# Three stages between the products: the step sizes and two head norms each move beside a product

## The chip, the cores and the metric

The kernel is one program on one core of a Trainium2 chip. The time is device microseconds of that core, for one call. The engines named below are PE (TensorE, matrix products; PEld is its weight load), ACT (ScalarE), DVE (VectorE), POOL (GpSimd) and SP (SyncE, which here issues the loads of weights).

## The reference, cut to what matters

The program computes three transformer layers in float32. The change touches the mixer of the third, which has two branches over the same normed tokens (H): an attention branch with output O and a state-space branch (a scan) with output Y. This is what the touched stages compute, written from the kernel:

```
O   = differential_attention(H)                 # 8 heads of 128 features, 512 tokens
O   = O / rms_over_each_head(O) * subln * 0.8   # the attention's head norm: 8 groups of 1 tile
dt  = softplus(H @ w_dt + dt_bias)              # 32 step sizes for each of 768 tokens
a   = -exp(a_log) * dt; its sums up to, after and over each chunk; exp of the sums
for g in 4 groups:
    B, C, x = silu(conv3(H @ xbc[g]))           # 4 tiles of 128 features
    Y[g] = scan(B, C, x, dt, the sums)          # uses dt and the sums from its first step on
Y   = Y * silu(H @ z)
Y   = Y / rms_over_groups_of_256(Y) * ssd_norm  # the scan's norm: 4 groups of 2 tiles
YA  = (O @ w_ba) * sigmoid(H @ gates[0:8])
YS  = (Y @ w_bs) * sigmoid(H @ gates[8:16]) + YA
```

Behind it come the output product, a router, experts and their combination.

## The kernel before, in words

All activations lie feature by feature: a tile is 128 features (partitions) by up to 512 latent and 256 context tokens. The program is a list of stages, built by `plan` (L2930). Each stage has one method for each engine. Behind each stage every engine signals that it is done and waits until all four are (`run` in `build`, L3020 to L3037; L3035 is the wait, and the profile writes DVEq L3035 or ACTq L3035 for whoever came last). So nothing of one stage overlaps the next, but for one thing: SP isn't held by this meeting. It runs ahead and loads weights into a ring of 8 slots of 512 KB as soon as PE has used what lay there (`ring_loads`, L202, whose issue is L211; it waits on `unit_used`).

The stages around the change, in order, with their lines:

- `DiffAttention` (L1762), which ends at ACT L1921.
- `GroupNorm` on O (L1620): for each of 8 groups ACT squares (L1673), PE multiplies by a matrix of ones to sum over the partitions (L1654), ACT takes the root (L1679), and DVE inverts it (L1695), multiplies by 0.8 (L1698) and scales the tile (L1702). Buffers are doubled.
- `StepSizes` (L1941): PE forms 48 small products (L1969, 128x32 out); DVE computes the softplus as a chain of short instructions (L2011 to L2042), with one exponential by ACT (L2001, L2002); PE forms 11 products for the sums (L1981); DVE copies them (L2044) and spreads them (L2047), ACT takes the exponentials (L2004), DVE weighs (L2050), PE turns four tiles (L1995) and DVE copies them out (L2052). Its 8 ring slots all hold `w_dt`.
- Four times `ConvLinear` (L991) and `Scan` (L2060). `ConvLinear` has 4 units here; a unit is one ring slot and one output tile: 8 products of 512 columns and 8 of 256 (L1021). ACT copies the tile (L1049), DVE convolves it (L1062, L1065, L1070), ACT takes silu (L1042). PE's unit j needs what ACT took of unit j-2.
- `GatedLinear` with z (L1707): 8 units of 8 products (L1729), ACT's silu (L1742), DVE's product (L1751).
- `GroupNorm` on Y: 4 groups of two tiles.
- `Linear` with `w_ba` (L459): 8 units (L500), ACT's copy (L516). Then `GatedLinear`, `Linear`, `GatedLinear` again.

A product of float32 stands as two records in the trace, so 8 products of a unit are 16 records. The order of the work on each engine is the order in which the methods issue it; there is no scheduler. ACT holds one table of functions at a time, and `ACT_TABLE_LOAD` is put straight ahead of the instruction that needs another one.

Of the kernel before, what the change touches and what calls it, by code (L numbers as in the profile page):

```python
# [27 lines left out]
P = 128  # L28
# [158 lines left out]
class Stage:  # L187
    def sync(self, sp): pass
# [270 lines left out]
class Linear(Stage):  # L459
# [3 lines left out]
    def __init__(self, k, w, n_tiles, rhs, dst, kt=KD, spans=(LAT, CTX), func=ACT.Copy, t0=0, d0=0, scale=1.0):  # L463
# [22 lines left out]
    def tensor(self, pe):  # L486
        k, upt = self.k, self.upt

        def unit(i, j):
# [13 lines left out]
            mm.then_inc(k.sig("unit_used").sem, 1)  # L503

        run_body(pe, self.n_units, self.body, unit)

    def scalar(self, act):
        k, upt = self.k, self.upt

        def unit(i, j):  # L510
            if j % upt != upt - 1:
                return
            t = j // upt
            act.wait_ge(k.sig("unit_used").sem, self.u0 + j + 1 + i * self.body)
# [3 lines left out]
            a.then_inc(k.sig("out_taken").sem, 1)  # L518

        run_body(act, self.n_units, self.body, unit)  # L520

# [469 lines left out]
class ConvLinear(Stage):  # L991
# [3 lines left out]
    def __init__(self, k, w, n_tiles, dst, cw, cb, off, spans=(LAT, CTX), pair=True, t0=0, head=()):  # L995
# [13 lines left out]
    def sync(self, sp):  # L1009
        ring_loads(self.k, sp, lambda i, j, c: self.w[i + j + self.t0, :, 0:c], self.u0, self.n)  # L1010

    def tensor(self, pe):
        k = self.k

        def unit(i, j):
# [7 lines left out]
            mm.then_inc(k.sig("unit_used").sem, 1)  # L1023

        run_body(pe, self.n, 8, unit)

    def scalar(self, act):
# [16 lines left out]
        def unit(i, j):  # L1044
# [6 lines left out]
            silu(i, j)  # L1051

        run_body(act, self.n, 8, unit)

    def vector(self, dve):
# [17 lines left out]

        for j, raw in enumerate(self.head):
# [7 lines left out]
        def unit(i, j):  # L1082
# [6 lines left out]
            if self.pair and j % 2 == 1:  # L1089
# [3 lines left out]
                                  self.cv[:, (j - 1) % 4, 0:self.end], self.cv[:, j % 4, 0:self.end], ALU.mult)  # L1093

        run_body(dve, self.n, 8, unit, k.dve, 16)


# [608 lines left out]

class GatedLinear(Stage):  # L1707


    def __init__(self, k, w, n_tiles, x, dst, func, off, add=None, t0=0):  # L1710
# [10 lines left out]
    def tensor(self, pe):  # L1721
        k = self.k

        def unit(i, j):
# [6 lines left out]
            mm.then_inc(k.sig("unit_used").sem, 1)  # L1731

        run_body(pe, self.n, 8, unit)

    def scalar(self, act):
        k = self.k

        def unit(i, j):
            act.wait_ge(k.sig("unit_used").sem, self.u0 + j + 1 + i * 8)

            act.wait_ge(k.sig("conv_done").sem, self.conv + j - 1 + i * 8)
            act.activation(self.buf[:, j % 2, :], k.ps[:, j % 2, :], self.func).then_inc(k.sig("out_taken").sem, 1)  # L1742

        run_body(act, self.n, 8, unit)

    def vector(self, dve):
        k = self.k

        def unit(i, j):
# [7 lines left out]
            a.then_inc(k.sig("conv_done").sem, 1)  # L1757

# [182 lines left out]
class StepSizes(Stage):  # L1941
# [16 lines left out]
    def sync(self, sp):  # L1958
# [3 lines left out]
    def tensor(self, pe):  # L1962
        k = self.k
        u, st = self.u0, k.sig("dt_steps")
        for j in range(8):
            pe.wait_ge(k.slot[(u + j) % SLOTS], slot_count(u + j))
        for t in range(NTT):
            for c in range(KD):
                mm = pe.matmul(k.ps[:, 0, t * 32:(t + 1) * 32], lhsT=k.H[:, c, t * P:(t + 1) * P],  # L1969
# [1246 lines left out]
```

## Time and profile before

| what | us |
|---|---|
| median of 3 runs | 4620.02 (4615.8 to 4622.53) |
| the profiled execution | 4637.23 |
| its span, first to last instruction | 4635.4 |
| PE busy in the span | 4149.1 (90%) |
| DVE / ACT busy in the span | 1192.1 / 891.5 |
| head norm of O, first square to the next stage's first product | 2960.18 to 2999.65 |
| step sizes, first product to the convolved product's first | 2999.65 to 3040.10 |
| norm of Y, end of z to the first product of w_ba | 3430.18 to 3453.51 |

The profile is of one execution, and times in it are microseconds from its first instruction. A row of the timeline gives start, duration, engine, line, operation, output and input, count, and in brackets how long the engine was idle before it and who released it. A row of the stretches gives for each engine its busy time and the number of its instructions, and PEclk, the mean granted clock of TensorE: 1.00 is 2.4 GHz and 0.50 is 1.2 GHz.

### The profile page before, as it was taken

How to read it: one execution, taken by the hardware profiler on the slowest of the kernel's cores; microseconds unless marked ns; L12 is line 12 of the kernel's file. 1: busy time of each engine (PE TensorE's matmuls, PEld its weight loads, DVE VectorE, ACT ScalarE, POOL GpSimd, SP SyncE). 2: the span in 40 equal slices, each digit the busy share in tenths (PEclk: the TensorE clock that was granted, in tenths of full speed). 3: DMA queues.
4: the chain of work that ended last, by engine and by line, in shares of the span. 5: the costliest groups of instructions: out<-in, count | busy, mean ns of one | idle time of the engine just before them, and what ended most of it. 6: DMA issues, size and time to landing. Idle time of an engine off the chain costs nothing. (4 is left out here: it accounts for less than half of the span.)

```text
span 4635.4 us, 37843 instructions
## 1 busy us (share of the span) xinstructions
PE 4149.1 (90%) x14084; PEld 2292.8 (49%) x14084; DVE 1192.1 (26%) x1918; ACT 891.5 (19%) x1856; POOL 318.0 (7%) x363
## 2 busy tenths in 40 slices
PE   6988999999999997999989998678889988999993
PEld 2445765555673432455445745455534474443441
DVE  1014333320222124023320314533420132111115
ACT  2105311100121111011110415322310031111110
POOL 0005100000000000000000003100000011110103
PEclk8998999999999998999999999779889989999996
DMA  5610111113211110342212207010012217999995
GB/s 222 247 70 14 37 59 50 54 43 137 97 46 43 41 43 27 105 168 73 77 60 70 79 28 295 0 55 32 23 46 77 68 55 312 409 395 378 397 407 209
DMA packets 134904, 584.89 MB, mean 126 GB/s; under 512 B 16688, under 2 KB 18736, under 8 KB 107136
## 3 DMA queue, kind: packets, MB, share of 16 engines
q1 hardware_dynamic: 103920, 478.02, 28.1%
q0 software_dynamic: 23088, 76.89, 4.4%
q10 hardware_dynamic: 7776, 28.32, 1.5%
q8 instruction: 83, 1.36, 0.1%
q14 instruction: 37, 0.30, 0.0%
HBM read 528.63 MB, written 66.06 MB: 128 GB/s over the span
## 5 line engine op out<-in xcount | busy, mean ns | idle before, releaser
L1021 PE MATMUL ps<-arena 128*128 128x512 f32 (+1 forms) x2432 | 861.6, 517 | 5.2 <-DVEq L3035 3.4
L1021 PEld LDWEIGHTS ps<-arena 128*128 128x128 f32 x2432 | 464.5, 191 | 401.4 <-issue 373.9
L756 PE MATMUL ps<-arena 128*128 128x256 f32 x2088 | 459.8, 381 | 8.1 <-ACT arena L786 4.2
L2693 PE MATMUL ps<-arena 128*64 128x512 f32 (+1 forms) x1152 | 397.0, 621 | 39.9 <-DMA arena<-w_gate_up 38.0
L756 PEld LDWEIGHTS ps<-arena 128*128 128x128 f32 x2088 | 397.1, 191 | 67.4 <-issue 4.9
L587 PE MATMUL ps<-arena 128*128 128x512 f32 (+1 forms) x1072 | 373.9, 508 | 28.2 <-ACTq L3035 11.8
L970 PE MATMUL ps<-arena 128*128 128x512 f32 x768 | 335.6, 599 | 10.6 <-DVEq L3035 9.4
L587 PEld LDWEIGHTS ps<-arena 128*128 128x128 f32 x1072 | 203.3, 191 | 203.9 <-issue 166.8
L500 PE MATMUL ps<-arena 128*128 128x512 f32 (+1 forms) x648 | 275.7, 587 | 25.2 <-DVEq L3035 18.0
L1729 PE MATMUL ps<-arena 128*128 128x512 f32 x640 | 280.2, 600 | 8.9 <-POOLq L3035 6.6
L2693 PEld LDWEIGHTS ps<-arena 128*64 128x64 f32 (+1 forms) x1152 | 151.1, 169 | 248.6 <-issue 246.1
L970 PEld LDWEIGHTS ps<-arena 128*128 128x128 f32 x768 | 147.3, 192 | 197.1 <-issue 184.2
L1062 DVE TENSOR_SCALAR arena<-arena 128x768 f32<-128x768 f32 (+1 forms) x104 | 64.9, 624 | 589.2 <-ACT arena L1049 547.6
L500 PEld LDWEIGHTS ps<-arena 128*128 128x128 f32 x648 | 124.6, 193 | 175.8 <-issue 146.2
L1729 PEld LDWEIGHTS ps<-arena 128*128 128x128 f32 x640 | 123.0, 193 | 166.3 <-issue 162.0
L2708 PE MATMUL ps<-arena 128*64 128x512 f32 (+1 forms) x576 | 195.4, 595 | 1.0 <-DVE arena L2815 1.0
L1049 ACT ACTIVATE arena<-ps 128x512 f32<-128x512 f32 (+1 forms) x152 | 72.9, 518 | 601.7 <-PE ps L1021 601.7
L1491 PE MATMUL ps<-arena 128*128 128x512 f32 (+1 forms) x448 | 154.9, 509 | 3.6 <-DVEq L3035 2.9
L2801 DVE TENSOR_TENSOR arena<-ps,arena 128x256 f32<-128x256 f32 x54 | 23.0, 426 | 428.3 <-ACT arena L2747 428.3
L321 DVE TENSOR_TENSOR arena<-ps,arena 128x16 f32<-128x16 f32 x18 | 2.3, 171 | 507.0 <-PE ps L311 467.8
L1751 DVE TENSOR_TENSOR arena<-arena 128x512 f32<-128x512 f32 (+1 forms) x40 | 27.8, 694 | 367.5 <-ACT arena L1742 367.5
L1491 PEld LDWEIGHTS ps<-arena 128*128 128x128 f32 x448 | 86.1, 193 | 72.9 <-issue 63.2
(331 smaller groups left out, 3754.2 us busy)
## 6 DMA issues: line engine op xcount, KB each, us to landing
arena<-w_gate_up SPq DMA_DIRECT2D x144, 1024.0 KB, 16.4
arena<-ada SPq DMA_DIRECT2D x144, 512.0 KB, 5.9
arena<-w_down SPq DMA_DIRECT2D x72, 1024.0 KB, 13.2
arena<-ffn_in SPq DMA_DIRECT2D x88, 512.0 KB, 3.3
y_rows<-arena POOLq DMA_DIRECT2D x8, 4096.0 KB, 47.4
y_rows<-arena ACTq DMA_DIRECT2D x54, 512.0 KB, 8.1
arena<-ffn_out SPq DMA_DIRECT2D x32, 512.0 KB, 3.6
arena<-ret_qk SPq DMA_DIRECT2D x16, 512.0 KB, 3.6
```

The costliest lines, as they stand in the source:

```text
L500: mm = pe.matmul(k.ps[:, 2 * s + t % 2, 0:w], lhsT=k.ring[:, u % SLOTS, (c % 8) * P:(c % 8 + 1) * P], rhs=self.rhs[:, c, o:o + w], start=c ...
L587: mm = pe.matmul(k.ps[:, 2 * s + t % 2, 0:w], lhsT=k.ring[:, u % SLOTS, (c % 8) * P:(c % 8 + 1) * P], rhs=self.rhs[:, c, o:o + w], start=c ...
L756: mm = pe.matmul(k.ps[:, n % 4, 0:w], lhsT=k.ring[:, u % SLOTS, (c % 8) * P:(c % 8 + 1) * P], rhs=x[:, c, o:o + w], start=c == 0, stop=c = ...
L970: mm = pe.matmul(k.ps[:, 4 + n % 4, :].rearrange("p (a b) -> p a b", a=4), lhsT=x[:, c, t * P:(t + 1) * P], rhs=k.ring[:, s0:s0 + 4, c * P ...
L1021: mm = pe.matmul(k.ps[:, 2 * s + j % 2, 0:w], lhsT=k.ring[:, u % SLOTS, c * P:(c + 1) * P], rhs=k.H[:, c, o:o + w], start=c == 0, stop=c = ...
L1049: a = act.activation(self.raw[:, j % 2, o:o + w], k.ps[:, 2 * s + j % 2, 0:w], ACT.Copy)
L1062: dve.tensor_scalar(cv[:, 0:self.end], raw[:, 0:self.end], cw[1], cb, ALU.mult, ALU.add).then_inc(k.dve.count(), 1)
L1491: mm = pe.matmul(k.ps[:, 2 * s + t % 2, 0:w], lhsT=k.ring[:, u % SLOTS, c * P:(c + 1) * P], rhs=k.H[:, c, o:o + w], start=c == 0, stop=c = ...
L1729: mm = pe.matmul(k.ps[:, j % 2, :], lhsT=k.ring[:, u % SLOTS, c * P:(c + 1) * P], rhs=k.H[:, c, 0:T], start=c == 0, stop=c == KD - 1)
L1751: a = dve.tensor_tensor(self.dst[:, i * 8 + j, :], self.buf[:, j % 2, :], self.x[:, i * 8 + j, :], ALU.mult)
L2693: mm = pe.matmul(k.ps[lo:hi, self.BANK[j], :], lhsT=m.xT[:, j, c, lo:hi], rhs=m.WG[slot][:, c, :], start=c == 0, stop=c == KD - 1)
L2708: mm = pe.matmul(k.ps[lo:hi, 4 + half, :], lhsT=m.hT[:, j, f * P + lo:f * P + hi], rhs=m.WD[slot][:, f, half * T:(half + 1) * T], start=f ...
```

## The change

Three stages leave the list. What they did is issued inside other stages:

- `StepSizes` is no stage any more. Its parts are called by the first `ConvLinear` (argument `steps`, group 0 alone): SP loads `w_dt` first (`load`); PE forms the 48 products before unit 0 (`product`), the sums behind unit 2 (`sum_up`) and the turning behind unit 3 (`turn`); DVE runs the chain before it convolves unit 0 (`sizes`), copies behind unit 1 (`spread`) and at the end (`take`); ACT takes the first exponential before unit 0 and the second behind unit 1. The results lie in PSUM banks 4, 5 and 6 instead of 0, 1 and 2.
- The norm of O is `NormBeside` (new) inside the `GatedLinear` with z: the table `when` puts groups 0 and 1 behind unit 0, and groups 2 to 7 behind units 1 to 6.
- The norm of Y is `NormBeside` inside the `Linear` with `w_ba`: groups 0 to 3 behind units 0 to 3.

In each such unit ACT squares before it takes the unit's result and takes the root behind it, PE sums behind the unit's products, and DVE scales behind its own work for the unit.

```
@@ Linear and GatedLinear, PE, behind the unit's products (unit j or tile t)
+            if self.norm is not None:
+                self.norm.sums(pe, j)
...
@@ the same, ACT, before and behind the unit's own instruction
+            if self.norm is not None:
+                self.norm.squares(act, t)
             act.wait_ge(k.sig("unit_used").sem, self.u0 + j + 1 + i * self.body)
...
+            if self.norm is not None:
+                self.norm.roots(act, t)
...
@@ the same, DVE, behind the unit
+            if self.norm is not None:
+                self.norm.scale(dve, j)
...
@@ ConvLinear, PE
+            if self.steps is not None and j == 2:
+                self.steps.sum_up(pe)
+
+        if self.steps is not None:
+            self.steps.product(pe)
         run_body(pe, self.n, 8, unit)
+        if self.steps is not None:
+            self.steps.turn(pe)
...
@@ ConvLinear, ACT
+            if self.steps is not None and j == 1:
+                self.steps.sum_exps(act)
+
+        if self.steps is not None:
+            self.steps.first_exps(act)
         run_body(act, self.n, 8, unit)
...
@@ ConvLinear, DVE
+        if self.steps is not None:
+            self.steps.sizes(dve)
...
+            if self.steps is not None and j == 1:
+                self.steps.spread(dve)
 
         run_body(dve, self.n, 8, unit, k.dve, 16)
+        if self.steps is not None:
+            self.steps.take(dve)
...
+class NormBeside:
...
+    def sums(self, pe, t):
+        k = self.k
+        for g in self.when[t]:
+            pe.wait_ge(k.sig("square_ready").sem, self.sq_b + g + 1)
+            if g >= 2:
+                pe.wait_ge(k.sig("root_ready").sem, self.sd_b + g - 1)
+            for n in range(self.per):
+                mm = pe.matmul(k.ps[:, 4 + g % 2, :], lhsT=k.c("ones"), rhs=self.sq[:, g % 2, n, :], start=n == 0,
+                               stop=n == self.per - 1)
+            mm.then_inc(k.sig("sum_ready").sem, 1)
...
-    add(GroupNorm(k, O, 8, 1, lambda t: k.vec("subln"), F + 8192, after=1.0 - LAM_INIT))
-    add(StepSizes(k, d["w_dt"], dt, steps, F + 9984))
-        add(ConvLinear(k, d["xbc"], 4, bufs, "scw", "scb", F + 9984 + 4 * N, pair=False, t0=4 * g))
+        add(ConvLinear(k, d["xbc"], 4, bufs, "scw", "scb", F + 9984 + 4 * N, pair=False, t0=4 * g,
+                       steps=sizes if g == 0 else None))
-    add(GatedLinear(k, d["z"], 8, Y, Y, ACT.Silu, F + 8192))
-    add(GroupNorm(k, Y, 4, 2, lambda t: k.vec("ssd_norm", t, t + 1), F + 8192))
+    norm = NormBeside(k, O, 8, 1, lambda t: k.vec("subln"), F + 16384, ((0, 1), (2,), (3,), (4,), (5,), (6,), (7,), ()),
+                     after=1.0 - LAM_INIT)
+    add(GatedLinear(k, d["z"], 8, Y, Y, ACT.Silu, F + 8192, norm=norm))
-    add(Linear(k, d["w_ba"], 8, O, YA, spans=(LAT,)))
+    norm = NormBeside(k, Y, 4, 2, lambda t: k.vec("ssd_norm", t, t + 1), F + 16384, ((0,), (1,), (2,), (3,), (), (), (), ()))
+    add(Linear(k, d["w_ba"], 8, O, YA, spans=(LAT,), norm=norm))
```

On PE, between the attention (L1852) and the first convolved product (L1021), this stands before: the sums of the norm's squares (L1654), the step products (L1969), the sums of the steps (L1981) and their turning (L1995).

```order
L1654 MATMUL ps<-arena 128x512 [waits root_ready,square_ready] x6
L1969 MATMUL ps<-arena 128x32 [waits slot_loaded0,slot_loaded7,slot_loaded1,slot_loaded6,slot_loaded2,slot_loaded5,slot_loaded3,slot_loaded4,stage_met]
L1969 MATMUL ps<-arena 128x32 x47
L1981 MATMUL ps<-arena 128x4x16 [waits dt_steps]
L1981 MATMUL ps<-arena 128x4x16
L1981 MATMUL ps<-arena 128x6x16
L1981 MATMUL ps<-arena 128x16
L1981 MATMUL ps<-arena 128x6x16
L1981 MATMUL ps<-arena 128x16
L1981 MATMUL ps<-arena 128x4x16
L1981 MATMUL ps<-arena 128x16 x4
L1995 MATMUL ps<-arena 128x128 [waits dt_steps]
```

And this stands there now (L1951 is the attention's last product, L2069 the step products, L1036 the convolved product's unit 0 and 1):

```order
L1951 MATMUL ps<-arena 128x256 x5
L2069 MATMUL ps<-arena 128x32 [waits slot_loaded0,slot_loaded7,slot_loaded1,slot_loaded6,slot_loaded2,slot_loaded5,slot_loaded3,slot_loaded4,stage_met]
L2069 MATMUL ps<-arena 128x32 x47
L1036 MATMUL ps<-arena 128x512 [waits out_taken,slot_loaded4]
L1036 MATMUL ps<-arena 128x512 x7
L1036 MATMUL ps<-arena 128x256 x8
L1036 MATMUL ps<-arena 128x512 [waits out_taken,slot_loaded5]
```

The norm's sums are gone from this place, the step products follow the attention directly, and the convolved product follows them with a wait for its slot; the sums of the steps come two units later.

On ACT, in the stage with z, this stands before (L1742 is the silu):

```order
L1742 ACT_TABLE_LOAD [waits conv_done,unit_used]
L1742 ACTIVATE arena<-ps 128x512 [waits stage_met]
L1742 ACTIVATE arena<-ps 128x512 [waits conv_done,unit_used] x7
L1673 ACTIVATE arena<-arena 128x512 [waits stage_met]
L1673 ACTIVATE arena<-arena 128x512 x3
```

And this now, for units 0 and 1 and the start of unit 2 (L1758 squares, L1837 is the silu, L1778 the root):

```order
L1758 ACTIVATE arena<-arena 128x512 [waits stage_met]
L1758 ACTIVATE arena<-arena 128x512
L1837 ACT_TABLE_LOAD [waits conv_done]
L1837 ACTIVATE arena<-ps 128x512 [waits unit_used]
L1778 ACT_TABLE_LOAD
L1778 ACTIVATE arena<-ps 128x512 [waits sum_ready] x2
L1758 ACTIVATE arena<-arena 128x512 [waits sum_ready]
L1837 ACT_TABLE_LOAD [waits conv_done]
L1837 ACTIVATE arena<-ps 128x512 [waits unit_used]
L1778 ACT_TABLE_LOAD [waits inverse_ready]
L1778 ACTIVATE arena<-ps 128x512 [waits sum_ready]
L1758 ACTIVATE arena<-arena 128x512 [waits sum_ready]
```

The roots and squares of the norm now stand between the silus, two table loads come into each unit, and the load ahead of a silu no longer has the wait for the unit's products (`unit_used`): that one stands at the silu itself.

## Rows read from the trace of the kernel before

**Rows 1.** The page: span, and busy time, share and instructions of PE.
```profile
span 4635.4 us, 37843 instructions
PE 4149.1 (90%) x14084; PEld 2292.8 (49%) x14084; DVE 1192.1 (26%) x1918; ACT 891.5 (19%) x1856; POOL 318.0 (7%) x363
```
**Rows 2.** Busy time by stretch, with granted clock.
```profile
core 0: us, PE busy (x) PEld busy (x) DVE busy (x) ACT busy (x) POOL busy (x), PEclk, DMA share, GB/s
2952.00:2960.20 8.20, 5.15 (x27) 3.65 (x25) 0.00 (x0) 2.50 (x7) 0.00 (x0) 1.00 0.00 0
2960.20:2969.00 8.80, 4.09 (x8) 1.27 (x8) 5.59 (x4) 5.49 (x9) 0.00 (x0) 1.00 0.00 0
2999.60:3020.40 20.80, 20.69 (x96) 20.55 (x96) 0.00 (x0) 0.00 (x0) 0.00 (x0) 0.50 0.00 0
3040.10:3044.10 4.00, 4.00 (x5) 1.85 (x6) 0.00 (x0) 0.00 (x0) 0.00 (x0) 0.50 0.01 4
3044.10:3083.70 39.60, 39.53 (x124) 23.18 (x122) 8.92 (x15) 6.47 (x11) 0.00 (x0) 1.00 0.12 40
3375.20:3428.90 53.70, 53.62 (x125) 23.37 (x123) 4.85 (x7) 5.52 (x9) 0.00 (x0) 1.00 0.21 69
3453.50:3457.10 3.60, 3.59 (x5) 1.52 (x6) 0.00 (x0) 0.00 (x0) 0.00 (x0) 0.50 0.00 0
3511.30:3575.00 63.70, 62.22 (x145) 27.40 (x146) 5.55 (x8) 6.08 (x9) 0.00 (x0) 1.00 0.23 74
```
**Rows 3.** Timeline, the head norm of O: its first and its last instructions.
```profile
2960.18 1.15 ACT L1673 ACTIVATE arena<-arena 128x512 f32<-128x512 f32 x2
...
2994.95 3.35 DVE L1695 RECIPROCAL arena<-arena 128x512 f32<-128x512 f32 x1
2998.34 0.43 DVE L1698 TENSOR_SCALAR arena<-arena 128x512 f32<-128x512 f32 x1
2998.80 0.75 DVE L1702 SCALAR_TENSOR_TENSOR arena<-arena 128x512 f32<-128x512 f32 x1
```
**Rows 4.** Timeline, the step sizes up to the convolved product.
```profile
2999.65 20.69 PE L1969 MATMUL ps<-arena 128*128 128x32 f32 x96 [14.82 <-DVEq L3035]
...
3020.45 0.36 DVE L2011 TENSOR_TENSOR arena<-ps,arena 128x192 f32<-128x192 f32 x1 [20.90 <-PE ps L1969]
...
3031.79 0.26 DVE L2042 TENSOR_SCALAR arena<-arena 128x192 f32<-128x192 f32 x1
...
3032.11 4.88 PE L1981 MATMUL ps<-arena 128*128 128x64 f32 x22 [11.77 <-DVE arena L2042]
...
3040.10 15.14 PE L1021 MATMUL ps<-arena 128*128 128x512 f32 x38 [0.81 <-DVEq L3035]
```
**Rows 5.** DMA issues from 3020.3 to 3020.6: xcount, KB each, us to landing.
```profile
arena<-xbc SPq DMA_DIRECT2D x1, 512.0 KB, 3.6
```
**Rows 6.** Timeline of ACT in the convolved product.
```profile
3053.65 1.28 ACT L1042 ACT_TABLE_LOAD   x1
3056.80 0.84 ACT L1042 ACTIVATE arena<-arena 128x768 f32<-128x768 f32 x1 [1.87 <-DVE arena L1070]
```
**Rows 7.** Timeline, ACT and DVE at the end of z.
```profile
3428.86 0.60 ACT L1742 ACTIVATE arena<-ps 128x512 f32<-128x512 f32 x1 [6.27 <-PE ps L1729]
...
3429.49 0.69 DVE L1751 TENSOR_TENSOR arena<-arena 128x512 f32<-128x512 f32 x1 [6.17 <-ACT arena L1742]
```
**Rows 8.** Timeline of PE: sums for Y's norm, the start of w_ba, a later stage's start.
```profile
3435.45 3.71 PE L1654 MATMUL ps<-arena 128*128 128x512 f32 x8 [0.21 <-ACT arena L1673]
3453.51 57.08 PE L500 MATMUL ps<-arena 128*128 128x512 f32 x128 [14.36 <-DVEq L3035]
...
3567.98 52.30 PE L500 MATMUL ps<-arena 128*128 128x512 f32 x121 [1.46 <-DVEq L3035]
```
**Rows 9.** Busy time of the router's products of 96 columns and of 64 columns.
```profile
3837.20:3844.60 7.40, 7.38 (x64) 7.22 (x64) 7.33 (x12) 0.00 (x0) 0.00 (x0) 1.00 0.01 2
3781.80:3801.80 20.00, 19.38 (x89) 18.43 (x90) 4.09 (x42) 4.40 (x7) 1.25 (x2) 0.50 0.16 53
```

More of the change, by code:

```diff
@@ L459, with __init__ @@
 class Linear(Stage):
-    def __init__(self, k, w, n_tiles, rhs, dst, kt=KD, spans=(LAT, CTX), func=ACT.Copy, t0=0, d0=0, scale=1.0):
+    def __init__(self, k, w, n_tiles, rhs, dst, kt=KD, spans=(LAT, CTX), func=ACT.Copy, t0=0, d0=0, scale=1.0, norm=None):
+        self.norm = norm
         self.k, self.w, self.n_tiles, self.rhs, self.dst, self.kt = k, w, n_tiles, rhs, dst, kt
@@ L518, in unit, with vector @@
             a.then_inc(k.sig("out_taken").sem, 1)
+            if self.norm is not None:
+                self.norm.roots(act, t)
         run_body(act, self.n_units, self.body, unit)
+    def vector(self, dve):
+        if self.norm is not None:
+            for t in range(self.n_tiles):
+                self.norm.scale(dve, t)
 def run_body(eng, n, body, unit, chain=None, per=0):
@@ L1009, in sync @@
     def sync(self, sp):
+        if self.steps is not None:
+            self.steps.load(sp)
         ring_loads(self.k, sp, lambda i, j, c: self.w[i + j + self.t0, :, 0:c], self.u0, self.n)
@@ L1731, in unit @@
             mm.then_inc(k.sig("unit_used").sem, 1)
+            if self.norm is not None:
+                self.norm.sums(pe, j)
         run_body(pe, self.n, 8, unit)
@@ L1738, in unit @@
         def unit(i, j):
+            if self.norm is not None:
+                self.norm.squares(act, j)
             act.wait_ge(k.sig("unit_used").sem, self.u0 + j + 1 + i * 8)
@@ L1742, in unit @@
             act.activation(self.buf[:, j % 2, :], k.ps[:, j % 2, :], self.func).then_inc(k.sig("out_taken").sem, 1)
+            if self.norm is not None:
+                self.norm.roots(act, j)
         run_body(act, self.n, 8, unit)
@@ L1757, in unit @@
             a.then_inc(k.sig("conv_done").sem, 1)
+            if self.norm is not None:
+                self.norm.scale(dve, j)
         run_body(dve, self.n, 8, unit, k.dve, 8 if self.add is not None else 0)
@@ L1938, in scalar @@
                 turn(i - 2)
-class StepSizes(Stage):
+class StepSizes:
     def __init__(self, k, w, dt, steps, off):
@@ L1956, in __init__, with load, product @@
         self.exped = k.sig("sum_exps").take(1)
-    def sync(self, sp):
+    def load(self, sp):
         ring_loads(self.k, sp, lambda i, j, c: self.w[0, :, 0:c], self.u0, 8, lambda j: 256)
-    def tensor(self, pe):
+    def product(self, pe):
         k = self.k
-        u, st = self.u0, k.sig("dt_steps")
+        u = self.u0
         for j in range(8):
@@ L2050, in vector, with take @@
         dve.tensor_tensor(self.win, self.exps[:, UP:UP + REST], self.dt.rearrange("p a b -> p (a b)"), ALU.mult)
+    def take(self, dve):
+        k, st = self.k, self.k.sig("dt_steps")
         dve.wait_ge(st.sem, self.steps + 7)
-        dve.tensor_copy(self.turned, k.ps[:, 2, :])
+        dve.tensor_copy(self.turned, k.ps[:, 6, :])
 UP, REST, ALL = LTT * 32, NTT * 32, LTT * 32
```

69 lines of the change are left out of this document (60 added, 9 removed).

## The prediction

> **What bounds the kernel now.** I read the page first: of a span of 4635.4 us PE is busy 4149.1, which is 90%, and no other engine is over 26% [rows 1]. So the time is PE's work and the places where PE stands idle, and the change can only win at such places. The stretches and the timeline show two of them around the change. From the end of the attention at 2960.18 to the first convolved product at 3040.10 lie 79.92 us [rows 3, 4]. First comes the head norm of O: DVE needs 3.35 us to invert, 0.43 to multiply by 0.8 and 0.75 to scale, one group after the other, eight times, and PE waits 14.82 us at its end [rows 3, 4]. Then come the step sizes: 20.69 us of small products at a granted clock of 0.50, 11.6 us of a DVE chain (3020.45 to 3032.05), 4.88 us of sums, and the copies behind them [rows 2, 4]. The other place is the norm of Y: DVE ends z at 3429.49 + 0.69 = 3430.18, and PE's first product of w_ba starts at 3453.51, 23.33 us later, after 14.36 us idle [rows 7, 8]. Against these stand stretches in which PE is full and the others nearly idle: in z DVE is busy 4.85 of 53.70 us and ACT 5.52 [rows 2]. There the norms would be hidden.
>
> **From the attention to the first convolved product.** What is left ahead of unit 0 is the 48 small products (96 records) and the load of its weights. At 0.50 the products took 20.69 us, 0.2155 us a record [rows 2]. Now they start where the clock is at 1.00: it was so before 2960.2 and stayed so to 2969.0, with PE busy 4.09 of those 8.80 us [rows 2]. I estimate 0.108 us a record at 2.4 GHz, half of the price at 1.2. The nearest row on that side is the router's 96 columns at 1.00, 7.38 us for 64 records, 0.115 each; on the other side 64 columns at 0.50 stayed there through 20 us [rows 9]. The whole product lies between 10.4 us (all at 1.00) and 20.7 (all at 0.50). I take about 4 us at 1.00, which is 37 records, and 59 records at 0.2155, 12.7 us: together 16.7. I choose a value nearer to the slow end because this same product, with PE busy 20.69 of 20.80 us, did not lift the clock in the trace, and so I don't expect it to hold it.
>
> The Trainium skill ("TensorE: Matmul & The Clock Gate", What's actually happening) says that the clock is throttled by default and that a busy PE releases it. By that rule a PE that is busy without a gap would stay at 2.4 GHz, and the product would cost 10.4 us. The trace speaks against it, since the clock stayed at 0.50 over 20.69 busy us; it is the second rival below.
>
> The weights of the convolved product can't come earlier: `w_dt` fills all eight ring slots, and they come free together at the product's end. Before, eight loads were issued there too, but under the chain. The first landed 3.6 us after its issue [rows 5]; now PE waits for it, 3.7 us with the start. The later ones have a unit of 10 us each to land. So the first convolved product starts 16.7 + 3.7 = 20.4 us behind the attention instead of 79.9: minus 59.5 us.
>
> **In the convolved product.** The sums are issued behind unit 2: 22 records, 4.88 us at 0.50 [rows 4]. The clock there is 1.00 (3044.10 to 3083.70) [rows 2], so half, plus 2.4 us; the upper bound is 4.9. The start at 0.50, which costs 4.0 us of slow products [rows 2], I leave as it is, to within 2 us, as it hangs on when the clock rises. The DVE chain, 11.6 us from the product's end, lies beside 3.7 us of loading and unit 0 (8 products of 512 and 8 of 256 columns, 16 records and 16 half records at 0.43, 10.3 us, plus its slow start, about 12). It ends 4 us before DVE is first needed. If this cover were gone, PE would wait at unit 2. Behind unit 2, ACT loads a table (1.28 [rows 6]) and takes an exponential of 448 columns (like the silu of 512, 0.60 [rows 7]), and it has PE's unit 3, 10.3 us, for that and its own unit 2. The load ahead of a silu stands free of its wait: at 3053.65 it ran at once, and the silu came at 3056.80 when DVE was done [rows 6]. The turning (8 records, at most 1.7 us at the step products' 0.2155) goes beside ACT's and DVE's work on unit 3, and DVE's last copy of 512 columns (like its 0.69 in z [rows 7]) beside ACT's last silu of 0.84 [rows 6]. I take nothing, bounded by 0 and 1.7.
>
> **z with the norm of O.** PE gets 8 products of 512 columns, 16 records. At 1.00 z's own records cost 53.62 / 125 = 0.429 us, which gives 6.9; the norm's own sums came at 3.71 / 8 = 0.464, which gives 7.4 [rows 2, 8]. I take plus 6.9. PE waits for ACT's square of a group, but ACT is early: counted from the end of a unit's products it has silu 0.60 [rows 7], table 1.28 [rows 6], root as long as the silu, square half of 1.15 [rows 3], which is 3.1 us, and PE comes for that square only after its sum (0.86) and the next unit (6.87). Two table loads in each unit make ACT 4.4 us of 7.7. DVE has 0.69 + 3.35 + 0.43 + 0.75 = 5.2 us of 7.7; unit 0 has two groups, 9.8 us, and the delay is gone in three units. `when` ends with group 7 behind unit 6, and unit 7 has no norm, so what follows PE's last product is 0.60 of ACT and 0.69 of DVE as before [rows 7], and the silu's table load is behind none of it, since the wait for the products stands at the silu: 0 us, and 1.3 if it doesn't work so.
>
> **w_ba with the norm of Y.** The stage between goes. Between two such stages some 0.1 us of meeting remains, so minus 23.2 us. PE gets 8 products again, plus 6.9. ACT needs one table here and DVE 3.35 + 2 x 0.75 in each of the first four units; all is done by the middle of the stage. Before, w_ba began with 3.59 us at 0.50 [rows 2]. Now it begins 1.46 us behind z's products, and at the like place at 3567.98, after 1.46 us idle, the clock stayed at 1.00 [rows 2, 8]. Minus 1.8 us, bounded by 0 and 1.8.
>
> **The sum.** -59.5 + 2.4 + 6.9 - 23.2 + 6.9 - 1.8 = -68.3 us. Against the profiled execution's 4637.23 that is 4568.9. That execution is 17.2 us over the median of the runs, and nothing in these stages says that it lies there; I subtract the same from 4620.02: 4551.7, say 4552. Everything later (the gated products, router, experts) is issued as before and moves as a whole.
>
> **The rivals.**
> - The small products and the convolved product's start all run at 1.2 GHz. For it: the same product did. Against it: the clock is at 1.00 where it begins. It gives 20.7 instead of 16.7 (+4.0), the sums at 4.88 (+2.5), w_ba's slow start kept (+1.8), a longer slow start of unit 0 (+1.5): 4562.
> - The clock stays at 1.00 through the products and the load's wait: -6.3 for the products, -2.0 for unit 0's slow half: 4543.
> - The chains aren't hidden: PE waits in z for squares, which would need ACT's 3.1 us to be issued behind PE instead of beside it. Seven units x 3.1, and DVE's last group of 4.5 us at the end: +26, 4578. For it: ACT changes tables twice a unit. Against it: the 4.6 us between the square's 3.1 and PE's 7.7, worked out above.
> - The other side, slower than before: the new stops between units bring TensorE down to 1.2 GHz in z and w_ba and keep it there. At 2.4 GHz the two take 2 x (55.0 + 6.9) = 123.8 us; at 1.2 twice that. 4552 + 124 = 4676. It makes the kernel slower once more than 68 of those 124 us run at half speed. Against it: the sums are products of 512 columns that follow without a gap.
> - The change doesn't do what it says: something in the code keeps the chain in front, for instance the softplus before unit 0 on PE as well. Nothing on PE's side waits for it before unit 2, so this has hardly a chance; it would give back 12 us, 4564.
>
> **How the numbers follow.** The forecast 0.70, all slow 0.10, all fast 0.11, not hidden 0.05, chain in front 0.02, slower 0.02. The range reaches to both clock cases with the runs' own spread (4615.8 to 4622.5, some 3 us): 4542 to 4564. A change of 0.2% is 9.2 us, about what a measurement of this kernel can tell from none; all cases but the last are faster by far more. Faster 0.97, same 0.01, slower 0.02.
>
> **What would show it.** In the profile after: the first convolved product about 20 us behind the attention's last ACT instruction, with PE idle 3 to 4 us and released by the load of xbc; the step products' 96 records between 10.4 and 20.7 us; z's PE stretch about 63.6 us without idle over 1 us inside; w_ba's start 1.5 us behind z's last product, at a clock of 1.00, and its stretch 62 us; no DVE wait in PE's rows for the norms' sums. I would be wrong if PE idles for `square_ready` or `root_ready` in z, if PE waits at unit 2 for DVE's chain, or if the clock falls inside z or w_ba.

## The result, and the profile after

The changed kernel took 4553.98 us (median of 4 runs, 4543.14 to 4561.47) where the kernel before took 4621.27 (4 runs on the same chip, 4615.8 to 4622.87). The ratio is 0.9856, with a 95% interval of 0.9842 to 0.9871: 1.44% faster. The forecast was 4552 with a range of 4542 to 4564. The profiled execution took 4561.47 us. Two executions of those reported below, one of the kernel with the norm of O alone (15255.1 us) and one of the kernel before (4753.46 us), ran with a lower granted clock and far above the rest, and are left out of all medians, ranges and ratios. The page of its profile has the span and the engines' busy time, to be read beside [rows 1]:

```profile
span 4559.6 us, 37841 instructions
PE 4122.5 (90%) x14084; PEld 2279.0 (50%) x14084; DVE 1191.9 (26%) x1918; ACT 908.6 (20%) x1870; POOL 318.5 (7%) x363
```

The span is 75.8 us shorter, and PE's busy time only 26.6: PE executes the same 14084 records, so the 49.2 us between the two are time in which it stood idle. ACT has 14 instructions more: the table loads that come from going to and fro between the norm's root and the stage's own function.

The timeline of PE from the attention's end to the scan, which answers to [rows 4] (start, duration, engine, line, operation, shapes, count, and in brackets the idle time before and who ended it):

```profile
2956.51 16.39 PE L2069 MATMUL ps<-arena 128*128 128x32 f32 x96 [0.58 <-POOLq L3152]
2976.63 33.72 PE L1036 MATMUL ps<-arena 128*128 128x512 f32 x96 [3.73 <-DMA arena<-xbc]
3010.19 2.52 PE L2084 MATMUL ps<-arena 128*128 128x64 f32 x22
3012.56 10.57 PE L1036 MATMUL ps<-arena 128*128 128x512 f32 x32
3022.96 0.60 PE L2101 MATMUL ps<-arena 128*128 128x128 f32 x4
3028.09 1.54 PE L2213 MATMUL ps<-arena 128*128 128x128 f32 x6 [4.52 <-ACTq L3152]
```

PE starts the step products at once behind the attention, waits once, 3.73 us, for the first load of `xbc`, and then not again until the stage ends. The sums (L2084) stand between unit 2 and unit 3 with no idle time ahead of them: DVE's chain was ready. The stretches of the same part, with PEclk, the granted clock, as the third value from the right:

```profile
2952.60:2956.40 3.80, 2.87 (x12) 2.19 (x12) 0.00 (x0) 0.79 (x3) 0.00 (x0) 1.00 0.00 0
2956.50:2961.20 4.70, 4.69 (x43) 4.70 (x43) 0.00 (x0) 0.00 (x0) 0.00 (x0) 1.00 0.01 3
2961.20:2972.90 11.70, 11.70 (x56) 11.56 (x55) 0.00 (x0) 0.00 (x0) 0.00 (x0) 0.50 0.00 0
2976.60:2981.70 5.10, 5.07 (x6) 2.19 (x7) 4.58 (x16) 0.00 (x0) 0.00 (x0) 0.50 1.02 419
2981.70:3023.00 41.30, 41.30 (x146) 25.63 (x145) 11.85 (x23) 9.47 (x13) 0.00 (x0) 1.00 0.19 68
```

The products began at 1.00, and 4.7 us in, with PE busy all the time, the clock fell to 0.50. It rose again 5.1 us into unit 0.

PE in z and at the start of `w_ba`, to be read beside [rows 8]:

```profile
3303.00 7.13 PE L1820 MATMUL ps<-arena 128*128 128x512 f32 x16 [0.87 <-DVEq L3152]
3309.97 1.88 PE L1768 MATMUL ps<-arena 128*128 128x512 f32 x4
3311.69 7.03 PE L1820 MATMUL ps<-arena 128*128 128x512 f32 x16
3318.55 1.02 PE L1768 MATMUL ps<-arena 128*128 128x512 f32 x2
...
3358.04 7.03 PE L1820 MATMUL ps<-arena 128*128 128x512 f32 x16
3366.53 7.15 PE L501 MATMUL ps<-arena 128*128 128x512 f32 x16 [1.46 <-DVEq L3152]
3373.51 1.88 PE L1768 MATMUL ps<-arena 128*128 128x512 f32 x4
```

The norm's sums (L1768) stand between the units, and none has a bracket. The list of PE's waits from 3303 to 3430 (who, how many us in all, how often, the longest) holds only the meetings of the stages:

```profile
PE ps L501 <- DVEq L3152: 1.5, 1, 1.5
PE ps L1820 <- DVEq L3152: 0.9, 1, 0.9
PE ps L1820 <- ACTq L3152: 0.7, 1, 0.7
```

And z and `w_ba` as stretches, to be read beside [rows 2]:

```profile
3303.00:3365.10 62.10, 62.07 (x144) 27.26 (x144) 40.89 (x31) 32.35 (x38) 0.00 (x0) 1.00 0.18 60
3366.50:3428.70 62.20, 62.17 (x144) 27.14 (x144) 19.08 (x12) 12.12 (x20) 0.00 (x0) 1.00 0.20 67
```

DVE is now busy 40.89 of 62.10 us in z and ACT 32.35, PE has 128 records of its own and 16 of the norm, and it is never without work. ACT's part around unit 1 shows how the two table loads of a unit lie:

```profile
3318.75 0.60 ACT L1837 ACTIVATE arena<-ps 128x512 f32<-128x512 f32 x1 [3.77 <-PE ps L1820]
3319.37 1.28 ACT L1778 ACT_TABLE_LOAD   x1
3320.66 0.60 ACT L1778 ACTIVATE arena<-ps 128x512 f32<-128x512 f32 x1
3321.16 0.62 ACT L1758 ACTIVATE arena<-arena 128x512 f32<-128x512 f32 x1
3321.80 1.28 ACT L1837 ACT_TABLE_LOAD   x1
3326.48 0.60 ACT L1837 ACTIVATE arena<-ps 128x512 f32<-128x512 f32 x1 [3.40 <-PE ps L1820]
```

Silu, the root's table, the root, the square of the next group, silu's table: 4.38 us, and then ACT waits 3.40 us for the next unit's products. The square is there at 3321.78, and PE asks for it only behind the products of the next unit.

**Where the time went.** The starts of the stages, read in the timelines of the two profiled executions, give this account (us; the last column is what was forecast):

| from, to | before | after | difference | forecast |
|---|---|---|---|---|
| first instruction behind the attention, first convolved product | 79.9 | 20.1 | -59.8 | -59.5 |
| convolved product, first scan | 48.5 | 51.5 | +3.0 | +2.4 |
| z, `w_ba` | 81.4 | 63.5 | -17.9 | -16.3 |
| `w_ba`, gates | 57.8 | 62.9 | +5.1 | +5.1 |
| sum of what the change touches | | | -69.6 | -68.3 |
| all else | | | -6.2 | 0 |

"All else" is three stretches whose instructions are the same in both kernels: the scans and the other convolved products came 8.6 us shorter, the end from the gates on 6.1 longer, and what lies ahead of the attention's end 3.7 shorter. In the scans and ahead of the attention's end the difference goes with how long TensorE stood at 1.2 GHz: in the scans 68.5 us of the one execution and 49.2 of the other, ahead of the attention's end 191.1 and 177.5. In the end stretch, from the gates on, it does not: 174.7 us at 1.2 GHz in the one and 175.0 in the other, and PE's busy time is within 1.1 us of the same, so that the 6.1 us are idle time of PE. Half of it (41.0 us for 38.0) is waiting for the experts' weights (`w_gate_up`); what set it the runs don't tell. A second profile of the changed kernel (below) had 44.4 us at 1.2 GHz in the scans and a span of 4544.8. By the same four rows it gives -57.4, +2.1, -17.9 and +5.1, together -68.1. So an account by stretches is good to a microsecond or two where the change is, and a single span is not.

### The profile page after: what moved, and what is told of

Its sections match the earlier page's. It is cut to its first block and busy times, and to the rows that moved or that the text cites. A ratio compares the mean times of both kernels' runs of the same rounds, so it can differ in the third digit from the quotient of the medians.

```text
span 4559.6 us, 37841 instructions
## 1 busy us (share of the span) xinstructions
PE 4122.5 (90%) x14084; PEld 2279.0 (50%) x14084; DVE 1191.9 (26%) x1918; ACT 908.6 (20%) x1870; POOL 318.5 (7%) x363
## 5 line engine op out<-in xcount | busy, mean ns | idle before, releaser
L1036 PE MATMUL ps<-arena 128*128 128x512 f32 (+1 forms) x2432 | 859.9, 516 | 8.0 <-DMA arena<-xbc 3.7
L1036 PEld LDWEIGHTS ps<-arena 128*128 128x128 f32 x2432 | 463.7, 191 | 402.6 <-issue 372.6
L290 PE MATMUL ps<-arena 128*2 128x512 f32 x576 | 73.0, 627 | 48.7 <-DMA arena<-ada 48.7
```

The lines of the kernel that those rows point to most:

```text
L290: mm = pe.matmul(k.ps[32 * j:32 * j + 2, self.bank, :], lhsT=self.cvec[:, 2 * c:2 * c + 2], rhs=k.ring[:, (u + j) % SLOTS, h * T:(h + 1) * ...
L1036: mm = pe.matmul(k.ps[:, 2 * s + j % 2, 0:w], lhsT=k.ring[:, u % SLOTS, c * P:(c + 1) * P], rhs=k.H[:, c, o:o + w], start=c == 0, stop=c = ...
```

## The experiments

Each was run with a profile, and timed in turns with the kernel before. Ratios are against the kernel before on the same chip, where it took 4624.07 us (first four) or 4625.06 (last four).

| kernel | median us | runs from, to | ratio | 95% interval |
|---|---|---|---|---|
| step sizes alone | 4607.28 | 4597.61, 4626.37 | 0.9965 | 0.9950 to 0.9979 |
| norm of O alone | 4587.66 | 4578.60, 4594.99 | 0.9928 | 0.9906 to 0.9950 |
| norm of Y alone | 4603.78 | 4596.73, 4611.85 | 0.9961 | 0.9948 to 0.9974 |
| whole change, `w_dt` outside the ring | 4551.58 | 4541.56, 4556.08 | 0.9840 | 0.9819 to 0.9862 |
| whole change again | 4546.66 | 4544.16, 4561.11 | 0.9836 | 0.9810 to 0.9862 |
| step products the other way round | 4540.16 | 4533.65, 4544.68 | 0.9818 | 0.9794 to 0.9842 |
| the same, and half the sums for Y | 4533.60 | 4528.02, 4536.72 | 0.9799 | 0.9775 to 0.9822 |
| whole change, each inverse of O twice | 4567.82 | 4554.16, 4582.04 | 0.9871 | 0.9845 to 0.9897 |

### One part at a time

The first three kernels each make one of the three moves and put the other two back as stages of their own.

The step sizes alone:

```
     add(DiffAttention(k, Q, K, V, O, d["y_rows"], F + 20480))
+    add(GroupNorm(k, O, 8, 1, lambda t: k.vec("subln"), F + 8192, after=1.0 - LAM_INIT))
...
-    add(GatedLinear(k, d["z"], 8, Y, Y, ACT.Silu, F + 8192, norm=norm))
+    add(GatedLinear(k, d["z"], 8, Y, Y, ACT.Silu, F + 8192))
+    add(GroupNorm(k, Y, 4, 2, lambda t: k.vec("ssd_norm", t, t + 1), F + 8192))
...
-    add(Linear(k, d["w_ba"], 8, O, YA, spans=(LAT,), norm=norm))
+    add(Linear(k, d["w_ba"], 8, O, YA, spans=(LAT,)))
```

> Only the step sizes move into the convolved product; both head norms are stages of their own again. Theory (a sum of independent places): the step products now start behind the norm of O, where the clock is at 0.50, so they take 20.7 us and not 16.4; the load's wait stays 3.7 us; so the first convolved product comes 24.4 us behind the norm instead of 40.45, and the sums add 2.5 us behind unit 2: 13.6 us less than before, 4607.7 us. Rival (the products lower the clock themselves and start fast anywhere): 16.4 us, 17.9 us less, 4603.4. Rival (the chain of 11.6 us isn't hidden): 2 us less, 4619.

PE's timeline of this kernel, and the stretch of the products with its clock:

```profile
2995.99 20.69 PE L2069 MATMUL ps<-arena 128*128 128x32 f32 x96 [14.82 <-DVEq L3151]
...
3020.40 29.89 PE L1036 MATMUL ps<-arena 128*128 128x512 f32 x83 [3.72 <-DMA arena<-xbc]
```

```profile
2995.90:3016.70 20.80, 20.69 (x96) 20.55 (x96) 0.00 (x0) 0.00 (x0) 0.00 (x0) 0.50 0.00 0
```

Behind the norm, where PE has stood idle 14.82 us, the products run at 0.50 throughout, as they did before [rows 4]. The gain is the chain's: 24.4 us from the products' start to unit 0 in place of 40.5. Up to the first scan it is 74.8 us in place of 88.9, 14.1 less where the theory says 13.6. So the trace decides against the first rival, by which the products would have taken 16.4 us here, and against the second, by which the chain would stand in front. The time alone (16 us less by the ratio, 10 to 23 by its interval) excludes only the second.

The norm of O alone:

```
-    sizes = StepSizes(k, d["w_dt"], dt, steps, F + 9984 + 10 * N)
+    add(StepStage(StepSizes(k, d["w_dt"], dt, steps, F + 9984)))    # load, product, sizes, sum_up, ..., take
...
-        add(ConvLinear(..., t0=4 * g, steps=sizes if g == 0 else None))
+        add(ConvLinear(..., t0=4 * g))
...
+    add(GroupNorm(k, Y, 4, 2, lambda t: k.vec("ssd_norm", t, t + 1), F + 8192))
...
-    add(Linear(k, d["w_ba"], 8, O, YA, spans=(LAT,), norm=norm))
+    add(Linear(k, d["w_ba"], 8, O, YA, spans=(LAT,)))
```

> Only the norm of O moves beside z; the step sizes are a stage again, directly behind the attention, and the norm of Y too. Theory: the norm's stage of 39.5 us goes, z gets 6.9 us of sums, and the step products start at a clock of 1.00 and take 16.4 us instead of 20.7, though nothing else about them changed: 36.9 us less than before, 4584.4 us. Rival (the products' shorter time belongs to their place in the convolved product's stage): they take 20.7 us, 32.6 less, 4588.7.

The same products directly behind the attention, and their stretches:

```profile
2958.17 18.89 PE L2069 MATMUL ps<-arena 128*128 128x32 f32 x96 [0.58 <-POOLq L3173]
```

```profile
2958.10:2960.10 2.00, 1.93 (x18) 1.96 (x18) 0.00 (x0) 0.00 (x0) 0.00 (x0) 1.00 0.03 8
2960.10:2977.20 17.10, 16.97 (x81) 16.83 (x80) 0.03 (x1) 0.00 (x0) 0.00 (x0) 0.50 0.00 0
```

They came between the two expectations: the clock fell here as well, but 2.0 us in, not 4.7. So the 16.4 us of the first profile was one draw, and 4 us of fast products is not a constant of the kernel. The median, 4587.66, lies nearer to the rival's 4588.7 than to the theory's 4584.4, but by the ratio's interval the gain is between 23 and 43 us, which doesn't tell them apart.

The norm of Y alone:

```
+    add(GroupNorm(k, O, 8, 1, lambda t: k.vec("subln"), F + 8192, after=1.0 - LAM_INIT))
...
+    add(StepStage(StepSizes(k, d["w_dt"], dt, steps, F + 9984)))
...
-    add(GatedLinear(k, d["z"], 8, Y, Y, ACT.Silu, F + 8192, norm=norm))
+    add(GatedLinear(k, d["z"], 8, Y, Y, ACT.Silu, F + 8192))
```

> Only the norm of Y moves, beside w_ba. Theory: 23.2 us of stage go, 6.9 us of sums come, and the start of w_ba at half clock (3.6 us) goes with it: 18.1 us less than before, 4603.2 us; the profile shows w_ba's start at a clock of 1.00. Rival (the slow start stays): 16.3 less, 4605.0.

The start of `w_ba` in the timeline, and the clock there:

```profile
3419.79 7.14 PE L501 MATMUL ps<-arena 128*128 128x512 f32 x16 [1.47 <-DVEq L3172]
```

```profile
3419.80:3424.00 4.20, 4.20 (x10) 1.99 (x11) 0.00 (x0) 1.12 (x2) 0.00 (x0) 1.00 0.26 104
```

1.47 us behind z and at 1.00: the slow start [rows 2] is gone with the stage that caused it. From the start of z to that of the gates this kernel takes 121.1 us where the one before takes 139.2, 18.1 less, which was the forecast for this part. The three ratios lie 0.35, 0.72 and 0.39% below one, together 1.46%, where all three moves made at once gave 1.44 and 1.64%. By the stretches the parts give 14.1, 36.5 (the norm of O alone: 41.8 less up to the first scan, 5.3 more from z's start to `w_ba`) and 18.1, together 68.7 us, against 69.6 and 68.1 for all three at once. So the parts add up to a microsecond or so. They are not quite independent: how long the step products take depends on what stands ahead of them, 20.69 us behind the norm's stage and 16.39 to 18.93 behind the attention.

### Is the wait for the weights worth anything?

`w_dt` takes all eight slots of the ring, so that `xbc` can be loaded only behind the last step product. This kernel gives `w_dt` 256 words a partition of its own:

```
-        ring_loads(self.k, sp, lambda i, j, c: self.w[0, :, 0:c], self.u0, 8, lambda j: 256)
+        sp.dma_start(self.wdt, self.w[0]).then_inc(self.k.sig("w_dt_loaded").sem, 16)
...
-                               rhs=k.ring[:, u % SLOTS, c * 32:(c + 1) * 32], start=c == 0, stop=c == KD - 1)
+                               rhs=self.wdt[:, c * 32:(c + 1) * 32], start=c == 0, stop=c == KD - 1)
```

> The changed kernel, but w_dt goes to a place of its own (256 words of each partition) with one load instead of filling all eight ring slots, so that the convolved product's weights are loaded under the attention. Theory (PE's 3.7 us of idle time behind the step products are the first load's time to landing): the idle time goes, 3.7 us less than the changed kernel, 4550 by its median of 4554, and the start at half clock stays as it is to within 2 us. Rival (PE's idle time there has another reason, such as DVE's chain or the clock): no change. The difference is near what can be told by times; the profile tells it: PE idle before the first convolved product under 0.5 us, or 3.7.

PE's timeline, then the stretches around the place where unit 0 follows:

```profile
2956.94 18.88 PE L2068 MATMUL ps<-arena 128*128 128x32 f32 x96 [0.50 <-ACTq L3151]
2975.63 33.09 PE L1036 MATMUL ps<-arena 128*128 128x512 f32 x96
```

```profile
2959.00:2975.60 16.60, 16.60 (x80) 16.60 (x80) 0.00 (x0) 0.00 (x0) 0.00 (x0) 0.50 0.00 0
2975.60:2979.40 3.80, 3.80 (x7) 1.73 (x7) 2.72 (x6) 0.48 (x2) 0.00 (x0) 0.50 0.00 0
```

The bracket is gone: unit 0 follows the products without a gap. From the first step product to the first scan this kernel takes 69.5 us; the changed kernel took 71.6 and 73.1 in its two profiles, whose difference is again where the clock fell. The second had the same 18.9 us of products as this kernel, and against it 3.6 us are won, the wait's 3.64. The ratios (0.9840, and 0.9856 and 0.9836) don't tell the kernels apart. Unit 0 still begins at 0.50 for 3.8 us: the slow start comes from the step products, not from the wait.

The changed kernel was run again beside the last three, on their chip:

> The changed kernel once more, beside the others of this call: 4554 us, within 5.

The median is 4546.66, 7.3 us under the 4554 and so outside the 5 expected: the medians of this one kernel differ by as much between two sets of runs, the ratios (0.9856 and 0.9836) by less.

```profile
2951.38 18.93 PE L2069 MATMUL ps<-arena 128*128 128x32 f32 x96 [0.61 <-POOLq L3152]
2973.95 32.81 PE L1036 MATMUL ps<-arena 128*128 128x512 f32 x96 [3.64 <-DMA arena<-xbc]
```

18.93 us of products, as in the two kernels above (and in the last kernel below): four of the five profiles in which the step products follow the attention have 18.9, and the first has 16.4.

### What lets the clock fall

The step products keep PE busy without a gap and the clock falls all the same. The theory says that it is the form of these products, 48 of 32 columns; the rival that it is the thin end of the attention ahead of them (PE busy 2.87 of 3.80 us, in the stretches above). This kernel keeps the place, has `w_dt` outside the ring as the one above, and turns the product round: the 32 step sizes become the output's partitions and the tokens its columns, so that 16 products of 512 and 256 columns do the work of 48 products of 32. The result lies the other way and is turned back behind unit 0.

```
-        for t in range(NTT):
+        for s, (o, w) in enumerate((LAT, CTX)):
             for c in range(KD):
-                mm = pe.matmul(k.ps[:, 4, t * 32:(t + 1) * 32], lhsT=k.H[:, c, t * P:(t + 1) * P],
-                               rhs=k.ring[:, u % SLOTS, c * 32:(c + 1) * 32], start=c == 0, stop=c == KD - 1)
+                mm = pe.matmul(k.ps[0:32, 4 + s, 0:w], lhsT=self.wdt[:, c * 32:(c + 1) * 32], rhs=k.H[:, c, o:o + w],
+                               start=c == 0, stop=c == KD - 1)
...
+        for t in range(NTT):                             # in turn_rows, called behind unit 0
+            mm = pe.transpose(k.ps[:, 6, t * 32:(t + 1) * 32], self.rows[0:32, t * P:(t + 1) * P], k.c("ident")[0:32, 0:32])
```

> The changed kernel with w_dt in a place of its own, and the step products the other way round: w_dt is the stationary side (32 columns) and the tokens move (512 and 256 columns), 16 products instead of 48; ACT copies the 32 rows out, and PE turns them behind unit 0 of the convolved product; DVE's chain starts there. Theory (the 48 products of 32 columns let the clock fall to 0.50, and then they and the start of the convolved product run at half speed): the 16 products take 10.3 us at a clock of 1.00 that doesn't fall, the convolved product starts at 1.00, the turning adds 0.7: against the changed kernel 3.7 (load) + 6.1 (products) + 2.5 (slow start) - 0.7 = 11.6 us less, 4542. Rival (the clock falls at this place for another reason, the attention's thin end): the 16 products and unit 0 run in part at half speed: 4 to 6 us less, 4549. Rival (DVE's chain, now behind unit 0, comes late for the sums): PE waits behind unit 2, up to 5 us given back.

PE's timeline, and the stretches with their clock:

```profile
2958.24 10.51 PE L2075 MATMUL ps<-arena 128*32 128x512 f32 x32 [0.50 <-ACTq L3171]
2968.67 10.59 PE L1036 MATMUL ps<-arena 128*128 128x512 f32 x32
2979.19 0.56 PE L2083 MATMUL ps<-arena 32*128 32x32 f32 x6
```

```profile
2958.20:2968.70 10.50, 10.46 (x33) 3.47 (x33) 0.00 (x0) 0.00 (x0) 0.00 (x0) 1.00 0.01 2
2968.70:3013.00 44.30, 44.30 (x157) 27.05 (x157) 19.17 (x43) 10.68 (x17) 0.00 (x0) 1.00 0.11 36
```

Behind the same attention the clock stays at 1.00 through the products and through unit 0, which takes 10.59 us; in the changed kernel three units took 33.72 and 32.81, of which a unit at 1.00 (10.57) leaves 12.6 and 11.7 for unit 0. From the first step product to the scan it is 60.1 us against 71.6 and 73.1, 11.5 and 13.0 less where 11.6 was expected. PE waits nowhere in it; DVE's chain, which now begins behind unit 0, is still hidden. Of this gain 9.4 us are the turning round alone (60.1 against the 69.5 of the kernel that only has `w_dt` outside the ring). The profile of the last version, below, repeats it: 10.51 us of products and 10.59 for unit 0, all at 1.00. So the rival falls: the attention's thin end alone does not bring the clock down. What the two versions don't separate is which part of the form does it, since not only the columns differ: the narrow products load weights without a break (PEld busy 16.60 of 16.60 us above) and the wide ones in 3.47 of 10.50. The median is 6.5 us under that of the changed kernel on the same chip: in the direction expected, and by less than the 11.6, which the spread of the runs (11 and 17 us from the fastest to the slowest) leaves room for. What is shown to the microsecond is the stretch.

The last version also lets DVE add the two squares of a group of Y, so that PE sums one tile and not two:

```
+                dve.tensor_tensor(self.sq[:, g % 2, 0, :], self.sq[:, g % 2, 0, :], self.sq[:, g % 2, 1, :], ALU.add)
...
-            for n in range(self.per):
-                mm = pe.matmul(k.ps[:, 4 + g % 2, :], lhsT=k.c("ones"), rhs=self.sq[:, g % 2, n, :], start=n == 0,
-                               stop=n == self.per - 1)
+            mm = pe.matmul(k.ps[:, 4 + g % 2, :], lhsT=k.c("ones"), rhs=self.sq[:, g % 2, 0, :], start=True, stop=True)
```

> As the flipped kernel, and in the norm of Y DVE adds the two squares of a group, so that PE forms 4 sums beside w_ba instead of 8. Theory (what moved beside PE's products costs exactly PE's own time): 4 products of 0.86 us fewer, 3.4 us less than the flipped kernel, 4538.6. Rival (PE now waits for DVE's addition): the additions of 0.7 us come before PE's unit ends, so up to 3.4 us are given back only if ACT's squares come late.

The one place in `w_ba` where PE now waits:

```profile
3371.79 1.13 PE L1775 MATMUL ps<-arena 128*128 128x512 f32 x2 [0.30 <-DVE arena L1792]
```

From `w_ba` to the gates it is 60.0 us where it was 62.9: 2.9 less of the 3.4 that the four products cost, 0.30 of the rest being that wait. At 4533.60 us this is the fastest version. Against the one above it isn't told apart by time (the medians lie 6.6 us apart, and the runs of each spread by 9 and 11), but all its runs are faster than all of the changed kernel's on this chip.

### How much cover z has

The forecast called DVE hidden because a group costs it 5.2 us of a unit's 7.7. This kernel inverts each group of O twice, the first time for nothing. It takes 3.35 us more of DVE a group, which makes 8.5, more than the 7.7. The expectation speaks of the inverse of the first result; the kernel that was run takes both of the same root, so that the norm of O is scaled as before and only DVE's work changes.

```
+            if self.per == 1:
+                dve.reciprocal(rs, self.sd[:, g % 2, :]).then_inc(k.dve.count(), 1)
+                dve.wait_ge(k.dve.sem, k.dve.value())
             dve.reciprocal(rs, self.sd[:, g % 2, :]).then_inc(k.sig("inverse_ready").sem, 1)
```

> The changed kernel, but in the norm of O DVE takes the reciprocal twice, the second of the first's result, so that the scaling is by the root and not its inverse: the output of the attention branch isn't the reference's. DVE's work for a unit of z rises from 5.2 to 8.6 us, over PE's 7.7. Theory (the norm is hidden as long as DVE has under 7.7 us of work in a unit): DVE now sets the pace, with 8 x 8.6 = 69 us and the two plain products: z takes 63.6 + about 7 us and the stage's end comes about 7 to 8 us later, 4561.5 us, and PE waits in z for out_taken or root_ready. Rival (the cover is far larger, as it's z's whole 63 us against DVE's total): under 2 us. Rival (the norm was on the path already): 8 x 3.35 = 27 us more.

PE's timeline, the start of z and of `w_ba`, and DVE's in z:

```profile
3304.31 7.13 PE L1823 MATMUL ps<-arena 128*128 128x512 f32 x16 [0.87 <-DVEq L3155]
...
3381.66 8.98 PE L501 MATMUL ps<-arena 128*128 128x512 f32 x16 [15.28 <-DVEq L3155]
```

```profile
3314.03 3.35 DVE L1787 RECIPROCAL arena<-arena 128x512 f32<-128x512 f32 x1 [1.15 <-ACT arena L1778]
...
3376.36 3.35 DVE L1789 RECIPROCAL arena<-arena 128x512 f32<-128x512 f32 x1
...
3380.88 0.69 DVE L1851 TENSOR_TENSOR arena<-arena 128x512 f32<-128x512 f32 x1
```

None of the three expectations gives this. The theory has the pace of DVE right and the amount and the place wrong: z took 77.4 us instead of 63.5, 13.8 more, and the 15.28 us idle brought the slow start of `w_ba` back, 1.8 more (64.7 against 62.9); together 15.7 where 7 to 8 were expected. The median is 21 above that of the changed kernel, the runs spreading by 28. What I had left out: DVE's first group can't begin before unit 0, its copy, the sum and the root are done: 3314.03, which is 9.7 us into the stage. From there the eight groups follow each other without a gap, a new one each 8.5 us, and z ends at 3381.57. PE hadn't waited inside z at all; the whole delay is paid at the stage's end. The sum comes out: a group costs DVE 3.35 twice, 0.43 and 0.75, 7.9 us, and 9.7 + 8 x 7.9 + 7 products of 0.69 = 77.7 us. For the changed kernel this means that its cover in z is smaller than a count of busy time (40.89 of 62.10) says, but not gone: by the same sum, with 4.5 us a group, 9.7 + 8 x 4.5 + 7 x 0.69 = 51 us of 62. That last figure is an estimate from these rows.

## Why the prediction was right

- **Attention's end to the convolved product, forecast 20.4 us, came 20.1.** Each of its terms came: the products 16.39 (forecast 16.7), the wait for `xbc` with the start 3.73 (3.7). The four other profiles in which they follow the attention had 18.9 for the products, so that my split at 4 us was near the first draw and 2.2 us low for the rest; that the term fits to 0.3 us is luck. It was right in kind: the clock fell within the products in all five. Of the two rows that I leaned on for it, the one with 64 columns is weaker than I read it: only 13.89 of its 20 us are those products, the rest has 128 columns.
- **The rule that I weighed there.** The clock fell to 0.50 with PE busy 4.69 of 4.70 us and stayed down through 11.70 us of 11.70 busy. The Trainium skill ("TensorE: Matmul & The Clock Gate", What's actually happening) says that a busy PE releases the throttle. Products of 512 and 256 columns kept the clock in the same place (10.51 us, all at 1.00, twice); the products of 32 columns lost it, in each of the five profiles, and here the measurement decides against the sentence. The rival that followed from the rule (4543) was wrong for this kernel; the two things that it wanted, products of 10.4 us and a unit 0 at 1.00, are what the version turned round shows (10.51 and 10.59).
- **The sums behind unit 2, forecast +2.4.** 2.52 us at 1.00. The stage as a whole took 3.0 more; its start at 0.50 lasted 5.1 us and not 4.0.
- **DVE's chain, forecast 11.6 us beside unit 0.** It took 10.3 and ended 7.3 us before DVE's first convolution, which I had put at 4: DVE's last instruction of the chain, and its next one, in the timeline:

```profile
2983.07 0.26 DVE L2151 TENSOR_SCALAR arena<-arena 128x192 f32<-128x192 f32 x1
2990.66 0.68 DVE L1087 TENSOR_SCALAR arena<-arena 128x768 f32<-128x768 f32 x1 [7.32 <-ACT arena L1070]
```

It is a table load (1.28) shorter than before, since no function of another table now comes between the attention's exponentials and its own.
- **z with the norm of O, +6.9, and the norm of Y's stage, -23.2.** Together they came at -17.9 and not -16.3. The 1.6 us are the slow start that z had before (its first 3.3 us at 0.51) and hasn't now, which my sum held to be the same. The change did not do that: with the whole change and `w_dt` outside the ring, z's first 6.1 us were at 0.50 again (its first unit took 10.20 us where it takes 7.13 in the first profile). z began at 0.50 in four of the ten profiles and at 1.00 in six, so these 1.6 us are a draw.
- **z's cover.** No wait of PE's for a square or a root, as forecast, and silu's table loads free of its wait: L1837's load ran at 3321.80 and was over 3.40 us before its products were done, and at z's end it ran at 3359.91, so that behind PE's last product came only 0.60 and 0.69.
- **`w_ba`, +6.9 and -1.8.** 62.9 for 57.8, +5.1, with the clock at 1.00 from its start.
- **The subtraction of 17.2 us for where the profiled execution lay.** Needed, and mostly for the reason given: the profile's span says -75.8, the medians -67.3, the touched stretches -69.6. Of the 8.5 us between the first two, 6.2 lie in stages that nobody touched.
- **The total.** Forecast -68.3; the stretches gave -69.6 and, in the second profile, -68.1, the medians -67.3. The mechanism is right term by term, but an agreement closer than 2 or 3 us is luck: the draws of the clock in the step products (2.5 us) and at z's start (1.6 us) are as large.

What stays open: why the clock fell 4.7 us into the products in one profile and 1.9 to 2.0 us in the four others. One thing differs ahead of them: in the attention's last products the clock stood at 0.50 for 3.4 us of the first profile (2944.1 to 2947.6) and for 6.8 us of the others (2936.2 to 2943.1 in the kernel run again). Whether that is the cause no run here tells. The two profiles of the products turned round had one of each kind ahead of them and kept 1.00.

## What to carry to other kernels

Where a norm stands between two products and the time is PE's, put it beside a product that doesn't need it, and count three things: PE's own sums, each engine's time of a unit, and the first moment at which the chain can begin, since the chain that was too slow here was paid for at the stage's end and not where it ran. Try a product with few output columns turned round, so that the tokens are its columns, even if its result must be turned back: here 16.4 to 18.9 us became 10.5, with what followed at full clock from its first record. For a change of 1% read the touched stretches of two profiles against each other, and leave the two spans for last.

## What the runs showed of the hardware that I had not expected

- A busy PE can lose its clock. 96 records of 32 columns without a gap: 4.7 us at 1.00 and then 11.7 at 0.50, or 1.9 to 2.0 and 16.6 to 17.1; behind 14.82 us of idle time all 20.69 at 0.50. 32 records of 512 and 256 columns in the same place, same attention ahead: 10.51 us at 1.00.
- The idle time alone is no sign either: 3.73 and 3.64 us of waiting in front of unit 0, or none, gave 5.1, 3.2 and 3.8 us of slow start, and 1.46 us in front of `w_ba` none.
- A table load costs ACT 1.28 us and nothing more here: at 3319.37 + 1.28 = 3320.65 the root follows at 3320.66. Going to and fro twice in each unit of z cost the kernel nothing.
